# Where the projection units land in PSUM, when the block inverse starts, and how the score products are formed, in a one-core RWKV-7 and MoBA layer

## The chip, the cores and the metric

The kernel runs on one core of one Trainium2 chip. The metric is the device time of one execution in microseconds (us). In the profile PE is TensorE's matrix multiply, PEld its weight load, DVE VectorE, ACT ScalarE, POOL GpSimd and SP SyncE, whose queue issues nearly all DMAs.

## The reference

One layer on x of 512 tokens by 1024, everything in float32. Cut to what matters here:

```python
h = rms_norm(x, norm_mix_g)
proj = h @ w_in
shift_part, q_b, k_b, v_b, gate_a, gate_b = _split(proj, ...)
shift_part = token_shift_mix(shift_part, mu_shift)   # p + mu * (prev - p)
y_a = rwkv7_time_mix(...) @ w_up_a                   # 8 heads of 64
y_b = moba_attention(q_b, k_b, v_b) @ w_up_b         # 8 heads of 64, causal, ALiBi
mixed = sigmoid(gate_a) * y_a + sigmoid(gate_b) * y_b
x = x + mixed @ w_o
x = x + (silu(g_ff) * u_ff) @ w_ffn_out              # SwiGLU of rms_norm(x)
return rms_norm(x, norm_final_g)
```

`rwkv7_time_mix` is a recurrence over the tokens with a delta-rule state per head. The kernel computes it in 4 chunks of 128 tokens, which needs the inverse of a unit triangular 128 by 128 matrix for each head and chunk. `moba_attention` comes, for 512 tokens and blocks of 256, to full causal attention over 512 keys.

## The kernel before

**Products.** Big products are made from split operands. A float32 operand is held as a high part (float32r) and a low part (the rest), and `three` (L1853 to L1857) issues hi*hi, hi*lo and lo*hi into one bank of PSUM. The weights of `w_in` come in units of 128 by 1024: SP loads a unit into `wraw` (2 slots), ACT copies out the high part (`split_hi`, L860), DVE subtracts for the low part (`split_lo`, L1320), PE takes it (`take`). ACT and DVE work LEAD = 3 units ahead of PE. SP may start a load only when DVE has split the unit two before it, and ACT waits for PE to have used the unit four before.

**Stage one: 15 shift units** (u = 0 to 14: lora, k, r, v columns). For each, PE runs 24 products of 512 columns (`project`) into one bank. ACT then writes the scaled bank to SBUF (`keep_part`, L910) and DVE adds the shifted part (`shift`, L1377, it increments `mixed_ready`). Before, the units alternate between the banks 4 and 5, so unit u waits for the `shift` of unit u - 2. Between the units stand small products: `lora` (after u = 3, 4), `key_norm` (after u = 4 to 7, banks 0 and 1), `key_products` (after u = 9 and 11, banks 2, 3, 6, 7: p even and odd; L1928). ACT and DVE copy these products to `Mfull` (`m_even` L967, `m_odd` L1409).

**Block inverse.** SP stores the 32 by 32 diagonal blocks of `Mfull` to DRAM (L559) and loads them back as `Mb` (L563). DVE eliminates them in 31 steps of two TENSOR_TENSOR each (`eliminate`, L1416 and L1418), and SP takes the result `Tb` through DRAM again (L571, L575) to `Tc`. `transposed` (L1426) follows, and from `Tc` and its transpose the 128 by 128 inverses are joined per chunk. DVE's order is written out by hand. Before, the elimination comes after all 15 shifts, with one `split_lo` ahead of each of the steps 0, 9, 17 and 24.

**Stage two: v_b** (units 15 to 18, `U_VB`), 4 banks at once, one per token tile (`VB_BANK` 7, 0, 5, 6), with `gate_rows` (L2152) after the first unit and `bonus_rows` (L2159) after the third. ACT copies the four banks to `V_b` (L1068) when the last unit is done.

**Stage three: 4 chunks**, each with the masked score products of the recurrence, the joining of the inverse, the state and the outputs, filled in with the units 19 to 26 (`U_QK`, q and k of the attention) by `fill`. The unit's bank is copied to `stage` (L1075) and stored to `qk_scratch`. In chunk 0 the first things ACT does are `split_hi` of unit 22, the `stage` copy, and V_tok, B_tok and K_tok (L977). PE's `fill(c, 1, 0, 2)` waits for B_tok.

**Stage four: 16 attention steps** (4 pairs of heads p, 4 query tiles t, m = 4p + t). In each step PE runs one gate unit (5.5 us of products), `attn_scores(m + 1)` (L2221), the transposes of the weights (L2232) and the values (L2244). Before, `attn_scores` is one float32 product per head, with K = 64 (the two heads on the partitions 0 to 63 and 64 to 127) and 128 * (t + 1) columns. The profile counts two instructions for each such float32 product. q and k of a pair are loaded from DRAM to `qkT`.

After that come the up projections, `w_o`, the SwiGLU (seven-product scheme on 128 by 256 products) and the last norm, which the change does not touch.

## Time and profile before

| | |
|---|---|
| median of 3 runs | 831.39 us (830.79 to 831.90) |
| the profiled execution | 832.74 us |
| its span, first to last instruction | 831.0 us |
| granted TensorE clock | 0.998 of 2.4 GHz |
| PE busy | 811.0 us (98%) |
| DVE, ACT, POOL busy | 501.1, 339.1, 143.5 us |
| DMA | 80.08 MB, mean 96 GB/s |

The span leaves out 1.7 us of the profiled execution's time that lie before its first and after its last instruction. Busy of PE counts each product until its modelled end; successive products overlap, so the start-to-start distance of two products is shorter than the duration of one.

### The profile page before, as it was taken

To read this page: it belongs to the slowest core of one execution; us is meant where nothing else is said; L and a number is where in the kernel's file an instruction comes from. 1 tells how busy PE (TensorE), PEld (TensorE's weight loads), DVE (VectorE), ACT (ScalarE), POOL (GpSimd) and SP (SyncE) were. 2 spreads that over 40 slices of the span, in tenths; PEclk is the share of its full clock that TensorE was granted. 3 is DMA by queue.
4 is the path that set the end of the run, shared out by engine and by line. 5 is a ranking of instruction groups with operands and counts; after the bars stand their busy time and mean duration, and the time that the engine had idled before them with its cause. 6 is when DMAs were issued, how large, how long until landed. Compare 5 with 4: busy or idle time off the path is not lost.

```text
span 831.0 us, 14188 instructions
## 1 busy us (share of the span) xinstructions
PE 811.0 (98%) x5417; PEld 668.2 (80%) x5417; DVE 501.1 (60%) x772; ACT 339.1 (41%) x554; POOL 143.5 (17%) x132
## 2 busy tenths in 40 slices
PE   5999999999999999999999999999999999999997
PEld 4677777687777777777888898999999998888885
DVE  5479859553454554454762767977877876433334
ACT  6578432333325424426432443443443444333332
POOL 3063880222242101101320074000000000000000
PEclk9999999999999999999999999999999999999999
DMA  5531340511143221223254153333333313322222
GB/s 159 165 92 51 77 152 26 140 42 51 40 146 97 77 77 52 76 77 102 76 193 135 40 150 115 108 97 101 111 91 101 114 37 101 119 86 99 102 76 102
DMA packets 122578, 80.08 MB, mean 96 GB/s; under 512 B 15057, under 2 KB 110338, under 8 KB 122530
## 3 DMA queue, kind: packets, MB, share of 16 engines
q1 hardware_dynamic: 122194, 79.13, 32.1%
q8 instruction: 34, 0.56, 0.3%
q10 hardware_dynamic: 144, 0.26, 0.1%
q14 instruction: 14, 0.11, 0.0%
q0 software_dynamic: 192, 0.02, 0.0%
HBM read 74.15 MB, written 5.24 MB: 96 GB/s over the span
## 4 chain that ended last, share of the span: by engine, by line
PE 91%; DVE 4%; ACT 3%; DMA 1%; issue 1%; POOL 0%; SPq 0%; ACTq 0%; POOLq 0%; DVEq 0%
PE PS L1855 26%; PE PS L1857 25%; PE PS L1856 25%; PE PS L1955 2%; PE PS L2221 1%; PE PS L2232 1%; PE PS L2244 1%; PE PS L2054 1%; DVE sq L1394 1%; DMA xt<-in_x_dram 1%; PE PS L2152 1%; PE PS L2055 1%; DVE w_lo L1320 1%; PE PS L1874 1%; PE PS L1998 1%
## 5 line engine op out<-in xcount | busy, mean ns | idle before, releaser
L1855 PE MATMUL PS<-hT_hi,w_hi 128*128 128x512 f32 (+2 forms) x640 | 236.9, 370 | 2.8 <-DVE rkvT L1377 2.0
L1857 PE MATMUL PS<-hT_hi,w_lo 128*128 128x512 f32 (+2 forms) x640 | 229.2, 358 | 0.0
L1856 PE MATMUL PS<-hT_lo,w_hi 128*128 128x512 f32 (+2 forms) x640 | 229.2, 358 | 0.0
L1320 DVE TENSOR_TENSOR w_lo<-wraw,w_hi 128x1024 fp32r<-128x1024 f32 (+1 forms) x89 | 121.7, 1368 | 62.7 <-ACT w_hi L860 60.2
L1855 PEld LDWEIGHTS PS<-hT_hi,w_hi 128*128 128x128 f32 (+1 forms) x640 | 120.2, 188 | 28.9 <-issue 10.9
L1857 PEld LDWEIGHTS PS<-hT_hi,w_lo 128*128 128x128 f32 (+1 forms) x640 | 120.3, 188 | 19.0
L1856 PEld LDWEIGHTS PS<-hT_lo,w_hi 128*128 128x128 f32 (+1 forms) x640 | 120.4, 188 | 17.3 <-issue 1.0
L860 ACT ACTIVATE w_hi<-wraw 128x1024 fp32r<-128x1024 f32 (+1 forms) x89 | 93.1, 1047 | 64.9 <-PE PS L1857 33.4
L1855 PE MATMUL PS<-w_hi,hid_hi 128*128 128x512 f32 x176 | 68.5, 389 | 0.0
L1856 PE MATMUL PS<-w_lo,hid_hi 128*128 128x512 f32 x176 | 68.5, 389 | 0.0
L1857 PE MATMUL PS<-w_hi,hid_lo 128*128 128x512 f32 x176 | 68.5, 389 | 0.0
L1855 PE MATMUL PS<-hS,w_hi 128*128 128x256 f32 x192 | 54.3, 283 | 0.0
L1856 PE MATMUL PS<-hS,w_hi 128*128 128x256 f32 x192 | 54.3, 283 | 0.0
L1857 PE MATMUL PS<-hS,w_lo 128*128 128x256 f32 x192 | 54.3, 283 | 0.0
L1732 DVE TENSOR_TENSOR hid_lo<-hid,hid_hi 128x512 fp32r<-128x512 f32 x22 | 15.2, 691 | 58.6 <-ACT hid_hi L1220 58.6
L1220 ACT ACTIVATE hid_hi<-hid 128x512 fp32r (+1 forms) x22 | 13.9, 630 | 70.9 <-PE PS L1857 70.9
L1116 ACT ACTIVATE PT<-PS 128x128 f32<-128x128 f32 (+3 forms) x32 | 12.3, 435 | 69.1 <-PE PS L2244 67.8
L1855 PEld LDWEIGHTS PS<-w_hi,hid_hi 128*128 128x128 f32 x176 | 33.0, 188 | 6.9
L1856 PEld LDWEIGHTS PS<-w_lo,hid_hi 128*128 128x128 f32 x176 | 33.0, 188 | 6.9
L1857 PEld LDWEIGHTS PS<-w_hi,hid_lo 128*128 128x128 f32 x176 | 33.0, 188 | 6.7
L1855 PEld LDWEIGHTS PS<-hS,w_hi 128*128 128x128 f32 x192 | 36.9, 192 | 0.0
L1856 PEld LDWEIGHTS PS<-hS,w_hi 128*128 128x128 f32 x192 | 36.9, 192 | 0.0
(296 smaller groups left out, 1406.4 us busy)
## 6 DMA issues: line engine op xcount, KB each, us to landing
wraw<-in_w_in_dram SPq DMA_DIRECT2D x82, 256.0 KB, 3.1
wraw<-in_w_ffn_out_dram SPq DMA_DIRECT2D x44, 256.0 KB, 2.8
wraw<-in_w_ffn_in_dram SPq DMA_DIRECT2D x40, 256.0 KB, 3.1
pair_a<-in_w_ffn_in_dram SPq DMA_DIRECT2D x24, 256.0 KB, 3.7
pair_b<-in_w_ffn_in_dram SPq DMA_DIRECT2D x24, 256.0 KB, 3.7
wraw<-in_w_o_dram SPq DMA_DIRECT2D x16, 256.0 KB, 2.9
xt<-in_x_dram SPq DMA_DIRECT2D x4, 512.0 KB, 5.5
qk_scratch<-stage SPq DMA_DIRECT2D x8, 256.0 KB, 3.1
```

The source lines that it names most:

```text
L860: act.activation(w_hi[:, fourth % NSPL, 0:n], wraw[:, s, 0:n], ACT.Copy).then_inc(w_hi_ready, 1)
L1116: act.activation(PT[:, e].rearrange("p a b -> p (a b)")[:, 0:n], PS[:, 6 + e, 0:n], ACT.Copy)\
L1220: act.activation(hid_hi[:, r:r + 1, :], hid[:, bass.ds(k, 1), :], ACT.Copy).then_inc(acthi_ready, 1)
L1320: dve.tensor_tensor(w_lo[:, q, 0:n], wraw[:, s, 0:n], w_hi[:, q, 0:n].bitcast(F32), ALU.subtract)\
L1394: dve.reciprocal(sq[:, p, :], sq[:, p, :]).then_inc(rinv_ready, 1)
L1732: dve.tensor_tensor(hid_lo[:, r:r + 1, :], hid[:, bass.ds(k, 1), :], hid_hi[:, r:r + 1, :].bitcast(F32), ALU.subtract).then_inc(actlo_read ...
L1855: pe.matmul(out_, a_hi, b_hi, start=start, stop=False)
L1856: pe.matmul(out_, a_hi, b_lo, start=False, stop=False)
L1857: return pe.matmul(out_, a_lo, b_hi, start=False, stop=stop)
L1874: return pe.transpose(PS[:, k, t * P:(t + 1) * P], xn[:, t, k * P:(k + 1) * P], ident[:])
L1955: ins = pe.matmul(PS[:, (q + odd) % 4, i * 2 * P:(i + 1) * 2 * P], (Bt if q < 4 else Kt)[r, p, cs], kkE_R[r, p, c, :, :].rearrange("p a b ...
L1998: ins = pe.matmul(PS[HD:P, 4 + half, i * HD:i * HD + HD], MT_rb[0:HD, h, 0, HD:P], Tm[0:HD, h, :], start=True, stop=True)
```

## The change

It has four parts.

- **Banks.** The shift units go to the banks of `SHIFT_BANK` (0, 5, 4, 5, 4, 5, 6, 7, 4, 5, 0, 1, 4, 5, 4). A unit waits for the `shift` of the last unit in the same bank. Units 6 and 7 wait for the sigmoids that read the lora banks, units 10 and 11 for the `key_norm` copies of the banks 0 and 1. In the first v_b unit each of the four banks has a wait of its own, in the order of tiles 0, 1, 3, 2; in the last one the four tiles are finished one after the other, and ACT copies each as it is finished (`vb_mm`).
- **Inverse.** `m_odd` of pairs 2 and 3 goes ahead of the `split_lo` of that turn, ACT does both `m_even` before both `a_mix`. DVE leaves its shift loop after u = 12, does the shift of unit 13 and begins the elimination. The low parts of the units 16 to 20 stand ahead of the steps 3, 5, 8, 13 and 21, the shift of unit 14 ahead of step 6, the low part of unit 21 after `bonus`.
- **Score products.** q and k of a pair are loaded as `qk_raw`, split by ACT (`pair_hi`) and DVE (`pair_lo`, in place), and `attn_scores` issues hi*hi, hi*lo and lo*hi for each head, the two heads in turn, over max(128 * (t + 1), 256) columns.
- **Order of loads.** SP loads pairs 0 and 1 ahead of the store of q/k column unit 6, and pairs 2 and 3 after eight more gate loads (2 units each of k = 2 and 3, two DMAs a unit), when the last RWKV output has been split.

The diff, without context that says nothing, the new semaphores, and the renaming of `shift_bank(u)` to `SHIFT_BANK[u]`:

```diff
@@ -87,6 +87,7 @@
 VB_BANK = [7, 0, 5, 6]
+SHIFT_BANK = [0, 5, 4, 5, 4, 5, 6, 7, 4, 5, 0, 1, 4, 5, 4]
@@ -261,7 +262,11 @@
         assert at[0] == Bt_at
-        qkT = sb("qkT", [P, 2 * NP_, T])
+        qk_at = at[0]
+        qk_raw01 = sb("qk_raw01", [P, 2, 2, T])
+        qk_hi01 = sb("qk_hi01", [P, 2, 2, T], F32R)
+        at[0] = qk_at
+        qk_lo01 = sb("qk_lo01", [P, 2, 2, T], F32R)
@@ -306,6 +311,14 @@
         assert at[0] <= top
+        qk_at = at[0]
+        qk_raw23 = sb("qk_raw23", [P, 2, 2, T])
+        qk_hi23 = sb("qk_hi23", [P, 2, 2, T], F32R)
+        assert at[0] <= top
+        at[0] = qk_at
+        qk_lo23 = sb("qk_lo23", [P, 2, 2, T], F32R)
+        qk_raw, qk_hi, qk_lo = [[t[:, p] for t in two for p in range(2)]
+                                for two in ((qk_raw01, qk_raw23), (qk_hi01, qk_hi23), (qk_lo01, qk_lo23))]
...
@@ -585,8 +597,7 @@
                     sp.wait_ge(qk_stored[i], 16 * (p + 1))
-                at_ = 2 * ((p + 1) % NP_)
-                sp.dma_start(qkT[:, at_:at_ + 2, :], qk_dram[2 * p:2 * p + 2].rearrange("n p t -> p n t"))\
+                sp.dma_start(qk_raw[p], qk_dram[2 * p:2 * p + 2].rearrange("n p t -> p n t"))\
@@ -594,15 +605,19 @@
                     load_cols(U_GATE + 1, U_GATE + 1, w_in, C_GB)
+                    sp.wait_ge(score_mm, 8 * TT)
+                    for p in range(NP_ // 2):
+                        load_pair(p)
                 store_qk(n)
-            sp.wait_ge(score_mm, 8 * TT)
-            for p in range(NP_ - 1):
-                load_pair(p)
             store_qk(2 * NP_ - 1)
-            load_pair(NP_ - 1)
             load_cols(U_GATE + 3, U_GATE + 3, w_in, C_GB + P)
-            with sp.Fori(1, KD // 2) as i:
+            for m in range(2):
+                load_gates(2 + m, U_GATE + 2 * m)
+            sp.wait_ge(yalo_ready, TT)
+            for p in range(NP_ // 2, NP_):
+                load_pair(p)
+            with sp.Fori(2, KD // 2) as i:
...
@@ -1029,6 +1044,8 @@
             for u in range(N_SHIFT):
+                if u == N_SHIFT - 2:
+                    keep_part(u)
@@ -1048,11 +1065,13 @@
                         m_even(p)
+                    for p in range(u - 10, u - 8):
                         a_mix(p)
+                if u != N_SHIFT - 2:
+                    keep_part(u)
                         row_scale(p)
-                keep_part(u)
@@ -1062,9 +1081,12 @@
                         gate_out(p)
-            act.wait_ge(w_used, U_VB + 4)
             for t in range(TT):
+                if t < TT - 1:
+                    act.wait_ge(vb_mm, t + 1)
+                else:
+                    act.wait_ge(w_used, U_VB + 4)
@@ -1074,6 +1096,10 @@
                                scale=1.0 if n % 2 else -HD ** -0.5).then_inc(fill_ready, 1)
+            def pair_hi(p):
+                act.wait_ge(qk_loaded[p], 16)
+                act.activation(qk_hi[p], qk_raw[p], ACT.Copy).then_inc(qkhi_ready, 1)
@@ -1090,6 +1116,8 @@
                     split_hi(U_QK + 2 * c + 1 + LEAD, U_QK + 2 * c + 1 + LEAD)
+                else:
+                    pair_hi(0)
@@ -1133,6 +1161,8 @@
                     ya_hi(TT - 1)
+                if n in (1, 5, 6):
+                    pair_hi((1, 5, 6).index(n) + 1)
...
@@ -1502,7 +1532,14 @@
-            for u in range(N_SHIFT):
+            def pair_lo(p):
+                dve.wait_ge(qkhi_ready, p + 1)
+                dve.tensor_tensor(qk_lo[p], qk_raw[p], qk_hi[p].bitcast(F32), ALU.subtract).then_inc(qklo_ready, 1)
+            for u in range(N_SHIFT - 2):
+                if u == 12:
+                    m_odd(2)
+                    m_odd(3)
@@ -1524,20 +1561,23 @@
                     key_rows(3)
-                if u in (10, 12):
-                    m_odd(u - 10)
-                    m_odd(u - 9)
+                    m_odd(0)
+                    m_odd(1)
+            shift(N_SHIFT - 2)
             for j in range(QB - 1):
-                if j in (0, 9, 17, 24):
-                    late = (0, 9, 17, 24).index(j)
-                    split_lo(U_VB + late + LEAD, U_VB + late + LEAD)
+                if j in (3, 5, 8, 13, 21):
+                    u = U_VB + 1 + (3, 5, 8, 13, 21).index(j)
+                    split_lo(u, u)
+                if j == 6:
+                    shift(N_SHIFT - 1)
                 bonus(p)
+            split_lo(U_QK + 2, U_QK + 2)
@@ -1555,6 +1595,7 @@
                 else:
+                    pair_lo(0)
@@ -1611,6 +1652,8 @@
                     ya_lo(TT - 1)
+                if n in (1, 5, 6):
+                    pair_lo((1, 5, 6).index(n) + 1)
@@ -1919,6 +1962,8 @@
                     pe.wait_ge(m_odd_ready, p - 1)
+                elif p:
+                    pe.wait_ge(mixed_ready, 8)
@@ -2129,9 +2174,15 @@
                 take(u)
-                if u >= 3:
-                    pe.wait_ge(mixed_ready, u - 1)
-                project(u, u, shift_bank(u), GH if u in (U_LORA + 1, U_LORA + 2) else P, fresh=0 if u == 0 else None)\
+                if u in (6, 7):
+                    pe.wait_ge(sg_ready, NP_)
+                    pe.wait_ge(a_ready, NP_)
+                elif u in (10, 11):
+                    pe.wait_ge(nrm2_ready, u - 7)
+                elif u >= 3:
+                    before = max(v for v in range(u) if SHIFT_BANK[v] == SHIFT_BANK[u])
+                    pe.wait_ge(mixed_ready, before + 1)
+                project(u, u, SHIFT_BANK[u], GH if u in (U_LORA + 1, U_LORA + 2) else P, fresh=0 if u == 0 else None)\
@@ -2162,18 +2213,19 @@
                 take(u)
-                if j == 0:
-                    pe.wait_ge(nrm2_ready, NP_)
-                    pe.wait_ge(mixed_ready, N_SHIFT - 1)
-                    pe.wait_ge(m_even_ready, NP_)
-                    pe.wait_ge(m_odd_ready, NP_)
-                for kk_ in range(2):
+                steps = [(kk_, t) for kk_ in range(2) for t in ((0, 1, 3, 2) if j == 0 else range(TT))]
+                if j == 3:
+                    steps = [(kk_, t) for t in range(TT) for kk_ in range(2)]
+                for kk_, t in steps:
+                    if j == 0 and kk_ == 0:
+                        pe.wait_ge(*((m_odd_ready, NP_), (mixed_ready, 11), (mixed_ready, 14), (m_even_ready, NP_))[t])
                     w = slice(512 * kk_, 512 * kk_ + 512)
-                    for t in range(TT):
-                        ts = slice(t * P, (t + 1) * P)
-                        ins = three(PS[:, VB_BANK[t], :], hT_hi[:, k, ts], hT_lo[:, k, ts], w_hi[:, q, w], w_lo[:, q, w],
-                                    k == 0, k == KD - 1)
+                    ts = slice(t * P, (t + 1) * P)
+                    ins = three(PS[:, VB_BANK[t], :], hT_hi[:, k, ts], hT_lo[:, k, ts], w_hi[:, q, w], w_lo[:, q, w],
+                                k == 0, k == KD - 1)
+                    if j == 3 and kk_ and t < TT - 1:
+                        ins.then_inc(vb_mm, 1)
@@ -2205,9 +2257,8 @@
                 p, t = m // TT, m % TT
-                a = 2 * ((p + 1) % NP_)
                 if t == 0:
-                    pe.wait_ge(qk_loaded[p], 16)
+                    pe.wait_ge(qklo_ready, p + 1)
@@ -2216,10 +2267,15 @@
                     pe.wait_ge(G_ready, 2 * TT)
-                for e in range(2):
-                    r = slice(HD * e, HD * e + HD)
-                    pe.matmul(PS[:, 2 + 2 * (m % 2) + e, 0:P * (t + 1)], qkT[r, a, t * P:(t + 1) * P],
-                              qkT[r, a + 1, 0:P * (t + 1)], start=True, stop=True).then_inc(s_done, 1)
+                w = max(P * (t + 1), TH)
+                parts = ((qk_hi, qk_hi), (qk_hi, qk_lo), (qk_lo, qk_hi))
+                for n, (q_part, k_part) in enumerate(parts):
+                    for e in range(2):
+                        r = slice(HD * e, HD * e + HD)
+                        ins = pe.matmul(PS[:, 2 + 2 * (m % 2) + e, 0:w], q_part[p][r, 0, t * P:(t + 1) * P],
+                                        k_part[p][r, 1, 0:w], start=n == 0, stop=n == 2)
+                        if n == 2:
+                            ins.then_inc(s_done, 1)
```

## Rows read from the trace of the kernel before

**Rows 1.** The page: busy time of the engines (part 1) and two groups (part 5).

```profile
PE 811.0 (98%) x5417; PEld 668.2 (80%) x5417; DVE 501.1 (60%) x772; ACT 339.1 (41%) x554; POOL 143.5 (17%) x132
...
L1320 DVE TENSOR_TENSOR w_lo<-wraw,w_hi 128x1024 fp32r<-128x1024 f32 (+1 forms) x89 | 121.7, 1368 | 62.7 <-ACT w_hi L860 60.2
...
L860 ACT ACTIVATE w_hi<-wraw 128x1024 fp32r<-128x1024 f32 (+1 forms) x89 | 93.1, 1047 | 64.9 <-PE PS L1857 33.4
```

**Rows 2.** Timeline of PE around its waits: start us, us, instruction [idle before <-releaser].

```profile
73.59 0.39 PE L1857 MATMUL PS<-hT_hi,w_lo 128*128 128x512 f32 x1
75.35 0.47 PE L1855 MATMUL PS<-hT_hi,w_hi 128*128 128x512 f32 x1 [1.36 <-DVE rkvT L1377]
...
89.35 0.47 PE L1855 MATMUL PS<-hT_hi,w_hi 128*128 128x512 f32 x1 [0.66 <-DVE rkvT L1377]
...
113.87 0.47 PE L1855 MATMUL PS<-w_hi,hT_hi 128*128 128x512 f32 x1 [0.28 <-issue]
...
145.90 0.39 PE L1857 MATMUL PS<-w_hi,hT_lo 128*128 128x512 f32 x1
147.07 0.47 PE L1855 MATMUL PS<-hT_hi,w_hi 128*128 128x512 f32 x1 [0.78 <-ACT V_b L1068]
```

**Rows 3.** Timeline of PE: a score step of 512 columns; split products of 256.

```profile
276.88 0.39 PE L1856 MATMUL PS<-hT_lo,w_hi 128*128 128x512 f32 x1
277.10 0.39 PE L1857 MATMUL PS<-hT_hi,w_lo 128*128 128x512 f32 x1
277.42 1.13 PE L2221 MATMUL PS<-qkT 64*128 64x512 f32 x4
278.48 0.77 PE L2232 MATMUL PS<-ident,Pr 128*128 128x128 f32 x5
...
560.11 0.28 PE L1857 MATMUL PS<-hT_hi,w_lo 128*128 128x256 f32 x1
560.23 0.28 PE L1855 MATMUL PS<-hT_hi,w_hi 128*128 128x256 f32 x1
```

**Rows 4.** Timeline of DVE: key copies, shift 13, first elimination step.

```profile
93.20 1.27 DVE L1409 COPY Mfull<-PS 128x512 f32<-128x512 f32 x2
...
112.91 0.75 DVE L1377 SCALAR_TENSOR_TENSOR rkvT<-PS,par,rkvT 128x511 f32<-128x511 f32 x1 [0.52 <-ACT rkvT L910]
...
118.05 1.28 DVE L1416 TENSOR_TENSOR outer<-Mb,Tb 128x31 f32<-128x31 f32 x1
119.37 0.21 DVE L1418 TENSOR_TENSOR Tb<-Tb,outer 128x31 f32<-128x31 f32 x1
```

**Rows 5.** Timeline of PE: the second group of key products.

```profile
94.99 2.06 PE L1928 MATMUL PS<-Bt,kkE_R 64*128 64x128 f32 x32
```

**Rows 6.** Busy time by stretch: us, PE, PEld, DVE, ACT, POOL, clock, DMA.

```profile
75.40:99.00 23.60, 22.94 (x145) 18.61 (x146) 23.43 (x20) 13.57 (x19) 13.57 (x9) 1.00 0.24 68
```

**Rows 7.** Timeline of POOL: its last work before chunk 0.

```profile
111.83 7.45 POOL L744 TENSOR_TENSOR rk<-rk,rkvT 128x512 f32<-128x512 f32 x4 [0.52 <-ACT rkvT L962]
```

**Rows 8.** Timeline of SP's queue: the inverse's way back, the next weights.

```profile
145.90 0.34 SPq L571 DMA_DIRECT2D t_scratch<-Tb  x1
...
150.87 10.47 SPq L511 DMA_DIRECT2D wraw<-in_w_in_dram  x6
```

**Rows 9.** Timelines of ACT and PE in chunk 0.

```profile
155.37 1.06 ACT L860 ACTIVATE w_hi<-wraw 128x1024 fp32r<-128x1024 f32 x1 [6.98 <-DMA wraw<-in_w_in_dram]
...
158.13 0.60 ACT L977 ACTIVATE B_tok<-PS 128x512 f32<-128x512 f32 x1
...
159.26 0.50 PE L1855 MATMUL PS<-hT_hi,w_hi 128*128 128x512 f32 x1
```

**Rows 10.** Busy time by stretch: stage four, columns as in Rows 6.

```profile
257.00:382.00 125.00, 124.80 (x684) 92.08 (x682) 62.82 (x154) 51.49 (x124) 13.54 (x10) 1.00 0.28 76
```

**Rows 11.** Timelines of ACT and PE at the end of chunk 3.

```profile
252.10 0.85 ACT L1000 ACTIVATE U_sb<-PS 128x256 f32<-128x256 f32 x2 [2.33 <-PE PS L2055]
...
256.69 0.49 PE L2221 MATMUL PS<-qkT 64*128 64x128 f32 x4
```

More of the change, by code:

```diff
@@ L415, in build @@
         yalo_ready = sem("yalo_ready")
+        vb_mm = sem("vb_mm")
         vb_ready = sem("vb_ready")
@@ L419, in build @@
         qk_loaded = [sem(f"qk_loaded{i}") for i in range(NP_)]
+        qkhi_ready = sem("qkhi_ready")
+        qklo_ready = sem("qklo_ready")
         alibi_ready = sem("alibi_ready")
@@ L474, in unit_width @@
             return KD * GH if isinstance(u, int) and u in (U_LORA + 1, U_LORA + 2) else 1024
-        def shift_bank(u):
-            return 4 + u % 2 if u else 0
         def cols(bank, shape, **k):
@@ L909, in keep_part @@
                     dst, i = rkvT[:, RKV_TILE[u - U_RKV], :], RKV_TILE[u - U_RKV]
-                act.activation(dst, PS[0:np_, shift_bank(u), :], ACT.Copy, scale=omu[0:np_, i:i + 1])\
+                act.activation(dst, PS[0:np_, SHIFT_BANK[u], :], ACT.Copy, scale=omu[0:np_, i:i + 1])\
                    .then_inc(tm_ready, 1)
@@ L1376, in shift @@
                 dve.wait_ge(tm_ready, u + 1)
-                dve.scalar_tensor_tensor(out=dst[:, 1:T], in0=PS[0:np_, shift_bank(u), 0:T - 1], scalar=mu,
+                dve.scalar_tensor_tensor(out=dst[:, 1:T], in0=PS[0:np_, SHIFT_BANK[u], 0:T - 1], scalar=mu,
                                          in1=dst[:, 1:T], op0=ALU.mult, op1=ALU.add).then_inc(mixed_ready, 1)
```

## The prediction

> **What bounds the kernel now.** I read the page's busy times first: PE is busy for 98% of the span, no other engine for more than 60% [rows 1]. So a microsecond is gained only where PE stands still or where its own work shrinks, and the next view is the list of PE's waits. Behind the first loads it stands still at four places that the change touches, and the timeline of PE gives each its price [rows 2]. The bracket is measured from the modelled end of the product before. Start to start is the better ruler: two split products of 512 columns follow each other at 0.23 us (276.88 to 277.10 [rows 3]), and from 73.59 to 75.35 it is 1.76, so 1.53 us are lost where the bracket says 1.36. The bracket is short by 0.17 each time. The four places:
>
> - 75.35, for the shift of unit 7: 1.53
> - 89.35, for the shift of unit 9: 0.66 + 0.17 = 0.83
> - 113.87, start of v_b, for the shift of unit 13, which ended at 113.66 [rows 4]: 0.28 + 0.17 = 0.45
> - 147.07, first fill of chunk 0, for the first copy of V_b: 1.17 - 0.23 = 0.94
>
> Together 3.75 us. Nearly everything else that PE does is its own work.
>
> **Banks.** Unit 9 now waits for the shift of unit 5, units 10 and 11 for copies that DVE made earlier, and both first stalls go: PE would be 1.53 + 0.83 = 2.36 us ahead at the second key products, which start at 94.99 [rows 5], so at 92.63. But they write banks that DVE's first `m_odd` must have read, and that copy starts at 93.20 and ends after half of 1.27, at 93.84 [rows 4]. Can it come earlier? Between 75.4 and 99.0 DVE is busy 23.43 of 23.60 us [rows 6]; the change reorders nothing there ahead of that copy, so no. PE starts at about 93.9, and of 2.36 us 1.09 are kept. That is what stands behind the stall: DVE is the bound of this stretch, and PE waits at the next place where they meet. Units 12 to 14 then follow without a wait, as before.
>
> **v_b.** The wait at 113.87 goes, since shift 13 is now done early (below): 0.45. In the last v_b unit the first token tile is finished after a quarter of 24 * 0.227 = 5.4 us, so ACT has copied it long before PE's first fill: 0.94. PE reaches chunk 0 1.09 + 0.45 + 0.94 = 2.48 us earlier.
>
> **The inverse.** When does it begin? PE's unit 13 ends at 113.87 - 0.45 - 5.44 - 1.09 = 106.9; latency 0.3, ACT's copy 0.67, the shift 0.75: 108.6, against 118.05 [rows 4], 9.4 us earlier. But POOL still has six TENSOR_TENSOR there: two of its last key rows and the four that take 7.45 us from 111.83 [rows 7]. The first elimination instruction took 1.28 us where its equal took 0.21, and ended at 119.33, 0.05 after POOL's last (111.83 + 7.45 = 119.28) [rows 4, 7]. A DVE instruction of this kind waits for the running POOL instruction. So until POOL is done, at about 117.5, DVE gets one short instruction for each of POOL's: 3 steps in 9 us instead of 1.3, 7.6 us lost. The Trainium skill (SBUF — State Buffer, Who interferes with whom) says the same and more sharply: a VectorE instruction with two SBUF inputs and a GpSimd one that reads SBUF exclude each other for the whole instruction, and the first to issue wins. The trace agrees (1.28 against 0.21), and by that rule too the head start is nearly spent.
>
> The end of the inverse, before at 145.90 [rows 8]: -9.4, +7.6, -1.07 for the block that is no longer at step 0, +2 * 1.37 for the low parts that come in (16, 17, 18, less 21; [rows 1]), +0.75 for shift 14: 146.5. I take 146, unchanged; without the blocking it would be 139. PE does not wait for it directly, but SP does: the weights of unit 22 are loaded only behind the inverse's DMAs, at 150.87, and their high part starts at 155.37 as the first thing of ACT in chunk 0 [rows 8, 9]. Behind it stand the stage copy, V_tok and B_tok: 155.37 + 1.06 + two starts of 0.5 + 0.6, so 157.9 at the earliest, and PE's fill that waits for B_tok wants to start at 159.26 - 2.48 = 156.8. A new stall, 1.1 us at most and nothing if the inverse ends over 1.1 us earlier. I take 0.8. Stages one to three give 2.48 - 0.8 = 1.7 us.
>
> **Low parts and loads moved.** Units 16 and 17 now get their low parts at about 118 and 121, and PE takes 16 after the gate rows, at about 124.5: covered by 5 us. Shift 14 at about 122.5 is what the last gate row needs at 123: covered by 0.5 us only. The bonus products on DVE end where they did, within 0.3 us of PE's need. SP's two early loads have no wait that is not over by then, and pairs 2 and 3 have several steps.
>
> **Score products.** A step of 512 columns takes PE 278.48 - 277.10 - 0.23 = 1.15 us [rows 3]. Split products of 256 columns follow at 0.12, of 512 at 0.227 [rows 3]: 0.107 per 256 columns and 0.013 fixed. The 16 float32 products of 128 columns at 94.99 take 2.06 [rows 5], 0.26 for the two heads of a pair: four passes of 0.053 and 0.04, so the two heads run side by side, or it would be over 0.43. For 512 columns four passes are 0.853, and 0.30 is fixed. By width that is 0.51, 0.73, 0.94 and 1.15, 3.33 a pair. Now there are three passes at 256, 256, 384 and 512 columns: 0.30 + 3 * (0.12, 0.12, 0.173, 0.227) = 0.66, 0.66, 0.82, 0.98, 3.12. Four pairs: 0.85 us gained. No row has a float32r product with K = 64. Bounds: heads one after the other add 4 * 3 * 0.64 = 7.7 us, so +6.8 in all; a fixed part of 0.2 instead of 0.3 in 16 steps gives 1.6 more. I take side by side, as the float32 rows show it.
>
> The splits cost ACT 1.05 and DVE 1.37 a pair [rows 1], hidden: in the attention DVE is busy 62.8 and ACT 51.5 of 125 us [rows 10]. Uncovered they would cost 2.4 us a pair. The tightest is pair 0: `U_sb` is done at 252.95, high part 254.0, low part 255.4, needed at 256.69 [rows 11]: 1.3 us to spare.
>
> **Sum.** 831.0 - 1.7 - 0.85 = 828.45 for the span, 830.2 with the 1.7 us around it. The profiled execution is 1.35 us above the median, so the median goes from 831.39 to 828.8.
>
> **Rivals.**
>
> *The head start of PE is lost at the inverse.* POOL holds DVE longer, shift 14 is late for the gate rows (0.5 us to spare) or the inverse ends 1 to 2 us later. Each late microsecond costs PE one, and beyond 1.4 us nothing of stages one to three is left: 831.39 - 0.85 = 830.5. For it: margins of 0.3 to 0.5 us. Against it: POOL has only six instructions left. Chance 0.17.
>
> *Heads one after the other.* If float32r products of two row groups do not overlap: 831.39 - 1.7 + 6.8 = 836.5, slower. It decides once the second head adds over 0.05 us to a slot (48 slots). Against it: the same placement overlaps in float32. Chance 0.08.
>
> *Weight loads bound the short slots.* Each slot needs two weight loads. If one takes the 0.12 us of the 256-column rows and they queue, a slot is 0.24, a step 1.02, a pair 4.08 against 3.33: +3.0, 832.7. Against it: at 94.99 there are 32 products with a load each in 2.06 us, 0.064 each [rows 5]. Chance 0.05. The Trainium skill (TensorE: Matmul & The Clock Gate, LDWEIGHTS) puts a load at its columns divided by 1.2, 107 ns for 128, an estimate by which this case would be 831.6; the trace's 64 ns speaks against it.
>
> **Chances.** The forecast has 0.70. The measurement can tell 0.2%, 1.7 us. Faster by more is below 829.7: 0.70. Within: 0.20 (the lost head start and the loads case). Slower: 0.10 (the serial heads, and a piece of the others). The range takes the forecast's own bounds (all 2.48 kept and the fixed part smaller: 827.2) and the lost head start (up to 831.3).
>
> **What would show it.** Right: no wait at units 9 and 11; the second key products at 93.9 behind the Mfull copy; the first elimination instructions over 1 us each from 108.6 on, and the inverse's end within 2 us of 145.9; a wait of PE for B_tok in chunk 0; score steps of 0.66 to 0.98 us. Wrong, if PE waits between 94 and 147 elsewhere, if the short eliminations run freely, or if a score step of 512 columns takes over 1.2 us.

## The result, and the profile after

The changed kernel takes 828.07 us (median of 6 runs, 826.93 to 828.95). The kernel before, run beside it, takes 832.1 (6 runs, 830.79 to 833.31). The ratio is 0.9949, 95% interval 0.9939 to 0.996. The forecast was 828.8, range 827.2 to 831.3, from a kernel before at 831.39.

The busy times of the changed kernel, from part 1 of its page, beside [rows 1]:

```profile
PE 807.7 (98%) x5449; PEld 669.6 (81%) x5449; DVE 509.7 (62%) x776; ACT 343.5 (42%) x558; POOL 141.2 (17%) x132
```

PE is busy 3.3 us less. ACT is busy 4.4 us more, the four high parts of q and k (4 * 1.05). DVE is busy 8.6 us more, and only 5.5 of them are the four low parts (4 * 1.37). The table of PE's waits comes next (line waited for: us in total, times, longest).

```profile
PE PS L1917 <- DVE xn L1368: 8.5, 2, 8.3
PE PS L1973 <- DVE Mfull L1439: 1.5, 1, 1.5
PE PS L2374 <- DVE xn L1695: 0.4, 1, 0.4
PE PS L2288 <- DVE Pr L1626: 0.2, 1, 0.2
PE PS L1898 <- ACT B_tok L992: 0.2, 1, 0.2
```

No line waits for `rkvT` or `V_b` any more: all four stalls of [rows 2] are gone. Two waits stand where the prediction put them, at the second key products (1.5) and for `B_tok` (0.2). Neither has quite the forecast size: the prediction's numbers leave 1.3 (2.36 - 1.09) for the first and 0.8 for the second.

**A ruler.** The two traces can't be subtracted as they stand. The first product of unit 0 starts at 16.71 us before and at 14.58 after:

```profile
16.71 0.49 PE L1855 MATMUL PS<-hT_hi,w_hi 128*128 128x512 f32 x1
```

```profile
14.58 0.47 PE L1898 MATMUL PS<-hT_hi,w_hi 128*128 128x512 f32 x1
```

Those 2.13 us lie in the loading and transposing of x, which the change doesn't touch: the last 16 transposes began 1.45 us earlier (12.54 against 13.99), and the product followed their start 0.7 us sooner. In the twelve kernels below, all with the same start, that product comes anywhere from 15.46 to 18.44. So places are counted from it from here on. Four lines of PE's timeline in the changed kernel answer to [rows 5], to [rows 2] and to [rows 11]:

```profile
91.89 2.06 PE L1973 MATMUL PS<-Bt,kkE_R 64*128 64x128 f32 x32 [1.53 <-DVE Mfull L1439]
...
142.49 0.39 PE L1898 MATMUL PS<-hT_hi,w_hi 128*128 128x512 f32 x1
...
154.82 0.47 PE L1898 MATMUL PS<-hT_hi,w_hi 128*128 128x512 f32 x1 [0.19 <-ACT B_tok L992]
...
252.01 0.39 PE L2275 MATMUL PS<-qk_hi 64*128 64x256 f32 x2
```

| from the first product of unit 0, us | before | after | gain so far |
|---|---|---|---|
| second key products | 94.99 - 16.71 = 78.28 | 91.89 - 14.58 = 77.31 | 0.97 |
| first fill of chunk 0 | 147.07 - 16.71 = 130.36 | 142.49 - 14.58 = 127.91 | 2.45 |
| first score product | 256.69 - 16.71 = 239.98 | 252.01 - 14.58 = 237.43 | 2.55 |
| end of the span | 831.0 - 16.71 = 814.29 | 825.2 - 14.58 = 810.62 | 3.67 |

The change is worth 3.67 us: 2.45 before chunk 0, 0.10 in the chunks, 1.12 from the attention on. The median fell by 4.0; the 0.4 between them is small beside the spread of the start.

The inverse, on DVE, POOL and SP's queue of the changed kernel:

```profile
106.50 1.32 DVE L1446 TENSOR_TENSOR outer<-Mb,Tb 128x31 f32<-128x31 f32 x1
107.86 0.22 DVE L1448 TENSOR_TENSOR Tb<-Tb,outer 128x31 f32<-128x31 f32 x1
108.11 1.18 DVE L1446 TENSOR_TENSOR outer<-Mb,Tb 128x60 f32<-128x60 f32 x1
109.32 1.34 DVE L1448 TENSOR_TENSOR Tb<-Tb,outer 128x60 f32<-128x60 f32 x1
110.70 1.25 DVE L1446 TENSOR_TENSOR outer<-Mb,Tb 128x87 f32<-128x87 f32 x1
111.98 1.34 DVE L1448 TENSOR_TENSOR Tb<-Tb,outer 128x87 f32<-128x87 f32 x1
113.35 2.19 DVE L1350 TENSOR_TENSOR w_lo<-wraw,w_hi 128x1024 fp32r<-128x1024 f32 x1
115.47 0.26 DVE L1446 TENSOR_TENSOR outer<-Mb,Tb 128x112 f32<-128x112 f32 x1
```

```profile
109.29 5.18 POOL L759 TENSOR_TENSOR rk<-rk,rkvT 128x512 f32<-128x512 f32 x4
```

```profile
142.48 0.34 SPq L583 DMA_DIRECT2D t_scratch<-Tb  x1
```

The first step begins at 91.92 instead of 101.34 on the ruler, 9.4 us earlier. Until POOL's multiplications end (109.29 + 5.18 = 114.47) five of the six short instructions take 1.18 to 1.34 us. The low part of 2.19 us spans that end, and behind it the next short instruction takes 0.26. The inverse is stored at 127.90 instead of 129.19, so 1.3 us are left of the 9.4.

### The profile page after: what moved, and what is told of

Read it like the earlier page. It is cut to its first block, busy times and chain, and to the rows that moved or that the text cites. A ratio compares the mean times of both kernels' runs of the same rounds, so it can differ in the third digit from the quotient of the medians.

```text
span 825.2 us, 14239 instructions
## 1 busy us (share of the span) xinstructions
PE 807.7 (98%) x5449; PEld 669.6 (81%) x5449; DVE 509.7 (62%) x776; ACT 343.5 (42%) x558; POOL 141.2 (17%) x132
## 4 chain that ended last, share of the span: by engine, by line
PE 90%; DVE 5%; ACT 2%; DMA 1%; issue 1%; POOL 0%; SPq 0%; ACTq 0%; POOLq 0%; DVEq 0%
PE PS L1898 26%; PE PS L1899 25%; PE PS L1900 25%; PE PS L2000 2%; PE PS L2288 1%; PE PS L2300 1%; PE PS L2275 1%; PE PS L2099 1%; DVE sq L1424 1%; DVE w_lo L1350 1%; PE PS L2203 1%; DMA xt<-in_x_dram 1%; PE PS L2100 1%; PE PS L2043 1%; PE PS L2073 1%
```

## Experiments

All twelve derive from the changed kernel. The ratio is to the kernel before, run beside each (its medians are 831.82 to 832.45 us). Places are from the first product of unit 0, as above, and each is the start of its row less that of the first product, in one trace of each kernel. "Key products" are the two groups of small products behind the units 9 and 11, "inverse stored" is the start of SP's store of `Tb`.

| kernel | median us | ratio to before (95%) | first product | first key products | second key | first fill | inverse stored | first score | end |
|---|---|---|---|---|---|---|---|---|---|
| before | 832.1 | 1 | 16.71 | 64.26 | 78.28 | 130.36 | 129.19 | 239.98 | 814.29 |
| after | 828.07 | 0.9949 (0.9939 to 0.996) | 14.58 | 62.61 | 77.31 | 127.91 | 127.90 | 237.43 | 810.62 |
| float32 scores | 830.08 | 0.997 (0.9958 to 0.9982) | 16.04 | 62.59 | 77.32 | 127.90 | 127.86 | 237.37 | 811.66 |
| head by head | 828.75 | 0.9958 (0.9943 to 0.9973) | 16.08 | 62.61 | 77.31 | 127.91 | 127.88 | 237.46 | 810.72 |
| exact width | 828.15 | 0.9946 (0.9932 to 0.9959) | 16.81 | 62.73 | 77.44 | 128.02 | 127.98 | 237.80 | 810.79 |
| two banks | 829.21 | 0.9968 (0.9956 to 0.998) | 15.69 | 64.22 | 78.25 | 128.83 | 127.91 | 238.33 | 811.51 |
| late inverse | 830.28 | 0.9974 (0.9963 to 0.9985) | 18.44 | 62.84 | 77.53 | 128.13 | 129.44 | 238.67 | 811.86 |
| quiet POOL | 828.8, one run | | 16.44 | 62.64 | 77.34 | 127.92 | 123.72 | 237.43 | 810.66 |
| copy first | 828.22 | 0.9956 (0.9942 to 0.9969) | 16.36 | 63.03 | 76.62 | 127.20 | 128.45 | 238.27 | 811.44 |
| copy first, early load | 827.29 | 0.9938 (0.9925 to 0.9952) | 16.47 | 62.64 | 76.24 | 126.81 | 127.82 | 236.29 | 809.43 |
| early load | 828.71 | 0.9958 (0.9944 to 0.9971) | 15.46 | 62.59 | 77.29 | 127.91 | 127.91 | 237.44 | 810.64 |
| all three | 826.66 | 0.9937 (0.9924 to 0.9951) | 15.63 | 62.63 | 76.20 | 126.78 | 127.85 | 236.25 | 809.27 |
| old last unit | 830.24 | 0.9969 (0.9956 to 0.9982) | 17.05 | 62.86 | 77.59 | 129.17 | 128.21 | 238.72 | 811.95 |
| late inverse, early load | 829.03 | 0.9957 (0.9942 to 0.9973) | 16.41 | 62.60 | 77.31 | 127.88 | 129.19 | 237.59 | 810.79 |

The column of the first key products is a second landmark. Up to there all but before and "two banks" run the same work, yet "late inverse", "old last unit" and "copy first" carry 0.23 to 0.42 us from unit 0, whose first one or two products take longer in these three traces. It is taken off where their later places are read. An interval is 0.9 to 1.3 us to each side, so the medians alone could not tell most of these kernels apart. The places agree within 0.1 us where nothing differs, but for such starts (0.12 in "exact width" too) and for the wait for `B_tok`, which varies by up to 0.4 us. The expected times below were reckoned from 828.07; most medians came 0.1 to 1.4 us above them, about as much as the intervals are wide, so the expectations are held against the places.

### Float32 score products

```diff
-                w = max(P * (t + 1), TH)
-                parts = ((qk_hi, qk_hi), (qk_hi, qk_lo), (qk_lo, qk_hi))
-                for n, (q_part, k_part) in enumerate(parts):
-                    for e in range(2):
-                        ...
+                w = P * (t + 1)
+                for e in range(2):
+                    r = slice(HD * e, HD * e + HD)
+                    pe.matmul(PS[:, 2 + 2 * (m % 2) + e, 0:w], qk_raw[p][r, 0, t * P:(t + 1) * P],
+                              qk_raw[p][r, 1, 0:w], start=True, stop=True).then_inc(s_done, 1)
```

> The changed kernel with each head's score product as one float32 product again, of the exact width, and without the high and low parts of q and k (loads, banks and order as changed). My theory: the attention gives back what three passes for four had saved: a step of 512 columns goes from 0.98 to 1.15 us, one of 128 from 0.66 to 0.51, and the stretch from the first score step to the last is 0.85 to 1.1 us longer; the time is 828.9 to 829.2 us. Rival: the gain of the attention comes from other moves (loads and gate copies in another order), then the stretch stays as in the changed kernel within 0.2 us.

From the first score product to the end it takes 811.66 - 237.37 = 574.29 us, the kernel before 574.31, the changed kernel 573.19. So this stretch is 1.10 us longer than in the changed kernel, as expected (0.85 to 1.1), and the end is 1.04 later on the ruler; the median is higher than expected, 830.08. The edit takes out the splits with the products, so the 1.1 us are the products less whatever the splits cost, and the other moves of loads and copies give nothing. The steps of PE alone give 1.04 (below), so the splits cost nothing that shows.

### Head by head

```diff
-                for n, (q_part, k_part) in enumerate(parts):
-                    for e in range(2):
+                for e in range(2):
+                    for n, (q_part, k_part) in enumerate(parts):
```

> The same six products of a score step, but the three of head 0 first and then the three of head 1, so that neighbours use the same 64 rows. My theory: two products lie side by side only where neighbours use different halves of the rows; a slot of two heads then costs twice its pass, a step of 512 columns 3 * 0.227 = 0.68 us more, of 384 0.52, of 256 0.36; a pair 1.9 us, four pairs 7.7 us, the time about 835.8 us. Rival: the order within a step makes no difference (the overlap is not one of neighbours), the time stays at 828.1.

My expectation fell. The end stands at 810.72, 0.1 from the changed kernel and far from the 7.7 us. Here are a step of 512 columns on PE and its weight loads. The program's order is three products of head 0 and then three of head 1:

```profile
273.79 0.39 PE L1900 MATMUL PS<-hT_hi,w_lo 128*128 128x512 f32 x1
274.11 0.50 PE L2275 MATMUL PS<-qk_hi 64*128 64x512 f32 x2
274.44 0.40 PE L2275 MATMUL PS<-qk_lo,qk_hi 64*128 64x512 f32 x2
274.68 0.40 PE L2275 MATMUL PS<-qk_hi,qk_lo 64*128 64x512 f32 x2
275.01 0.87 PE L2288 MATMUL PS<-ident,Pr 128*128 128x128 f32 x6
```

```profile
274.11 0.19 PEld L2275 LDWEIGHTS PS<-qk_hi 64*128 64x128 f32 x2 [0.35 <-issue]
274.22 0.20 PEld L2275 LDWEIGHTS PS<-qk_lo,qk_hi 64*128 64x128 f32 x2
274.45 0.19 PEld L2275 LDWEIGHTS PS<-qk_hi,qk_lo 64*128 64x128 f32 x2
```

Each row holds two instructions, one of each head: both heads load and multiply the same part together, although two other products stand between them in the program. The first product of head 1 starts 0.010 us behind the first of head 0 (0.003 where they are neighbours) and over 0.2 us before the second of head 0. The step takes 275.01 - 273.79 = 1.22 us, as with the heads interleaved (1.21). Each half of the rows runs its own sequence, and the order across halves didn't matter here. The Trainium skill (TensorEngine Tiling (Array Packing), Key Properties) says that different tiles can load weights and multiply in parallel, and the trace agrees: two heads, one slot of 0.24 us. The rival of serial heads, which I gave 0.08, doesn't come about in either order.

### Exact width of the first score product

```diff
-                w = max(P * (t + 1), TH)
+                w = P * (t + 1)
```

> The score products of the first tile of each pair take 128 columns instead of being widened to 256. By columns (0.107 us for 256 and 0.013 fixed) a pass falls from 0.12 to 0.067 us, 0.16 a pair and 0.65 us in all: 827.4 us. Rival: a float32r product of 128 columns is slower by column than one of 256; were it as slow as float32 (four passes of 0.053), a slot would take 0.22, 0.3 us more a pair and 1.3 us more in all: 829.4 us.

From the first score product to the end it takes 572.99 us against 573.19: 0.2 gained, not 0.65 and not a loss. The end itself stands no earlier (810.79), because the first score product came 0.37 us later in this trace, behind a slower start (0.12) and a wait of 0.6 for `B_tok`; the median is 828.15, not 827.4. Here are the step of 128 columns on PE and its loads:

```profile
282.82 0.39 PE L1900 MATMUL PS<-hT_hi,w_lo 128*128 128x512 f32 x1
283.14 0.33 PE L2275 MATMUL PS<-qk_hi 64*128 64x128 f32 x2
283.30 0.28 PE L2275 MATMUL PS<-qk_lo,qk_hi 64*128 64x128 f32 x2
283.41 0.28 PE L2275 MATMUL PS<-qk_hi,qk_lo 64*128 64x128 f32 x2
283.62 1.09 PE L2288 MATMUL PS<-ident,Pr 128*128 128x128 f32 x8
```

```profile
283.13 0.19 PEld L2275 LDWEIGHTS PS<-qk_hi 64*128 64x128 f32 x2 [0.35 <-issue]
283.24 0.19 PEld L2275 LDWEIGHTS PS<-qk_lo,qk_hi 64*128 64x128 f32 x2
283.35 0.19 PEld L2275 LDWEIGHTS PS<-qk_hi,qk_lo 64*128 64x128 f32 x2
```

The products follow at 0.16 and 0.11, where 256 columns gave 0.22 and 0.12. The loads follow at 0.11 and 0.11 here; at 256 columns the third came 0.12 behind the second, at the pace of the products. I read from this that at 128 columns the load sets the slot. Only the first product gains by the smaller width: a step takes 0.80 us instead of 0.87.

This corrects a step of the prediction. I had divided the 2.06 us of [rows 5] by 32 loads, read 0.064 us for one and held it against the figure of the Trainium skill (TensorE: Matmul & The Clock Gate, LDWEIGHTS: columns divided by 1.2, 107 ns for 128). But those 32 loads ran in the two halves of the rows side by side. Here one load takes 0.11, and the trace agrees with that figure. The rival failed for another reason: a slot's two loads don't queue, and 0.11 lies just under the 0.12 of 256 columns. The prediction's 831.6 let the two loads of a slot queue: that premise failed, not the figure.

### Two banks

```diff
-SHIFT_BANK = [0, 5, 4, 5, 4, 5, 6, 7, 4, 5, 0, 1, 4, 5, 4]
+SHIFT_BANK = [0, 5, 4, 5, 4, 5, 4, 5, 4, 5, 4, 5, 4, 5, 4]
...
-                if u in (6, 7):
-                    ...
-                elif u >= 3:
+                if u >= 3:
```

> The changed kernel with the projection units alternating between two PSUM banks again, each waiting for the shift before the last (unit 0 in bank 0). My theory: both stalls return (1.5 at unit 7, 0.8 at unit 9), but the 1.5 us that PE waits at the second key products for the copy of Mfull goes, so PE loses only 0.9 to 1.1 us by there and the same at the end: 829.1 us. Rival: the copy moves with the banks as well and all 2.36 us are lost: 830.4.

The two stalls are back (2.0 us in the table of waits) and the wait at the second key products is gone:

```profile
PE PS L1898 <- DVE rkvT L1407: 2.0, 2, 1.4
```

The second key products come at 78.25, 0.94 later than in the changed kernel, and the end 0.89 later. Of 2.36 us of stall, the further banks return 0.9. The copy of `Mfull` sits at 76.45 with two banks and at 76.48 with the six of `SHIFT_BANK`: DVE bounds this stretch.

### Late inverse

```diff
-            for u in range(N_SHIFT - 2):
+            for u in range(N_SHIFT):
...
-                if j in (3, 5, 8, 13, 21):
-                    u = U_VB + 1 + (3, 5, 8, 13, 21).index(j)
-                    split_lo(u, u)
-                if j == 6:
-                    shift(N_SHIFT - 1)
+                if j in (0, 9, 17, 24):
+                    late = (0, 9, 17, 24).index(j)
+                    split_lo(U_VB + late + LEAD, U_VB + late + LEAD)
```

(The shift of unit 13 and the low part of `U_QK + 2` behind the bonus fall away as well.)

> The changed kernel with the inverse begun behind the last shift again and with the low parts of units 16 to 21 where they were before the change (banks, split of the last v_b unit and score products as changed). My theory: POOL's multiplications had taken most of the head start, so without it the inverse ends only about 1.3 us later, counted from the first product of unit 0 (129.2 instead of 127.9 us), and PE loses 0.45 at the start of v_b for shift 13 and waits up to 1 us more for B_tok: 0.5 to 1.3 us in all, 828.6 to 829.4. Rival: the head start of some 10 us is real, the inverse ends 7 us or more later and PE loses 5 us or more.

With the 0.23 us of the start taken off, the inverse is stored 1.3 us later and the first score product comes 1.0 later; PE waits 1.2 us for `B_tok` instead of 0.2. The 0.45 us at the start of v_b didn't return, although shift 13 is late again. Shift 13 on DVE and the first product of v_b on PE:

```profile
114.24 0.73 DVE L1407 SCALAR_TENSOR_TENSOR rkvT<-PS,par,rkvT 128x511 f32<-128x511 f32 x1
```

```profile
114.43 0.39 PE L1894 MATMUL PS<-w_hi,hT_hi 128*128 128x512 f32 x1
```

The product starts 0.5 us before the shift ends, and without a wait: each token tile there now waits for its own bank, and the tile in the bank of unit 13 is taken last. The head start of 9.5 us (first step at 101.4 instead of 91.9, with the 0.23 off) is worth 1.3 on DVE and 1.0 on PE.

### Quiet POOL

```diff
-                pool.tensor_tensor(rk[:, p, :], rk[:, p, :], rkvT[:, p, :], ALU.mult).then_inc(rk_ready, 1)
+                pool.memset(rk[:, p, :], 0.0).then_inc(rk_ready, 1)
```

> POOL's four multiplications of rk by r for the bonus are replaced by memsets of the same tiles; this leaves the bonus term out of the result. My theory: they exclude DVE, so the elimination's short instructions that took 1.2 to 1.3 us beside them take 0.2 to 0.3, the low part beside them 1.4 instead of 2.2, and the inverse ends about 4 us earlier (counted from the first product of unit 0: 124 instead of 127.9); PE gains at most the 0.19 us that it waits for B_tok. Rival: the first steps are long for a reason of their own (first use of the tiles, chained waits), and stay over 1 us.

This kernel leaves the bonus term out of the result, and there is one time and one trace of it. DVE and POOL:

```profile
108.61 1.18 DVE L1448 TENSOR_TENSOR Tb<-Tb,outer 128x31 f32<-128x31 f32 x1
109.82 1.33 DVE L1446 TENSOR_TENSOR outer<-Mb,Tb 128x60 f32<-128x60 f32 x1
111.19 0.22 DVE L1448 TENSOR_TENSOR Tb<-Tb,outer 128x60 f32<-128x60 f32 x1
111.44 0.25 DVE L1446 TENSOR_TENSOR outer<-Mb,Tb 128x87 f32<-128x87 f32 x1
```

```profile
108.38 1.32 POOL L746 TENSOR_TENSOR rk<-aT,rkvT 128x512 f32<-128x512 f32 x1
109.78 1.29 POOL L748 TENSOR_TENSOR Kt<-rk,Kt 128x512 f32<-128x512 f32 x1
111.13 0.99 POOL L759 MEMSET rk<- 128x512 f32 x2
```

Beside POOL's last two TENSOR_TENSOR the short instructions take 1.18 and 1.33 and end 0.08 to 0.09 us behind them; beside the memsets they take 0.22 and 0.25. The inverse is stored 4.2 us earlier (4 expected), and PE gains nothing: 810.66. Its 0.19 us for `B_tok` is gone, but it waits 0.3 for `TmT`, a tile of the joining of the inverse in chunk 0, a little further on. That wait has the same 0.3 whether the inverse is stored at 123.72 (here) or at 129.19 ("late inverse, early load"), so it isn't a wait for the end of the elimination. The exclusion is shown, and also that in this range nothing of PE behind `B_tok` hangs on when the inverse is stored. The Trainium skill (SBUF — State Buffer, Who interferes with whom) says that a VectorE instruction with two SBUF inputs contends with a GpSimd one that reads SBUF and not with one that only writes it; the trace agrees on both halves.

### Copy first, with and without the early load, and the early load alone

On DVE the low part of unit 13 goes behind the copies. On SP unit 22's weights go ahead of the inverse's transfers:

```diff
-                split_lo(u + LEAD, u + LEAD)
+                if u != 10:
+                    split_lo(u + LEAD, u + LEAD)
...
                     m_odd(0)
                     m_odd(1)
+                    split_lo(u + LEAD, u + LEAD)
```

```diff
-            for n in range(3):
+            for n in range(4):
                 load_qk(n)
...
             for n in range(3, 2 * NP_):
-                load_qk(n)
+                if n > 3:
+                    load_qk(n)
```

> The changed kernel with DVE's low part of unit 13 behind the key rows 2 and 3 and the first two copies of Mfull instead of ahead of them. The wait of 1.5 us at the second key products goes, since the copy comes 1.9 us earlier. My theory: the gain doesn't last, since the weights of unit 22 come no earlier: the wait for B_tok in chunk 0 grows from 0.2 to 1.2 to 1.7 us, and the time is 827.6 to 828.1. Rival: the inverse and with it the load move up as far as PE does, the gain of 1.5 us stays: 826.6.

> As the run with the copy first, and SP issues the weights of unit 22 ahead of the transfers of the inverse instead of behind them. My theory: no wait for B_tok is left in chunk 0, so the 1.5 us of the second key products stay, and the 0.2 for B_tok comes on top: 826.4 us. Rival: the copies of B_tok wait for something other than the high part of unit 22 (the inverse itself, or PE's transposes), then the time is that of the run without the early load.

> The changed kernel with the weights of unit 22 loaded ahead of the inverse's transfers, and nothing else. My theory: only the wait of 0.19 us for B_tok is there to be gained, the first score step comes 0.1 to 0.2 us earlier counted from the first product of unit 0 (237.3), and the time is 827.9 us: the load helps only a PE that is ahead. Rival: the early load is worth the 1.7 us by which the run with the copy first and the early load came ahead of the one with the copy first alone; then 826.6.

*Copy first.* PE's wait at the second key products falls to 0.4. The copy came 1.1 us earlier, not 1.9: without the low part ahead of them, the two key rows on DVE ran beside POOL and took 3.0 us instead of 2.4:

```profile
89.19 3.04 DVE L1433 TENSOR_TENSOR kkE_R<-kk,kkE_R 128x512 f32<-128x512 f32 x2
92.16 1.27 DVE L1439 COPY Mfull<-PS 128x512 f32<-128x512 f32 x2
```

PE's waits of this kernel:

```profile
PE PS L1900 <- ACT B_tok L992: 1.8, 1, 1.8
...
PE PS L1975 <- DVE Mfull L1439: 0.4, 1, 0.4
```

The gain is not only lost, as I expected, but overpaid: with the 0.42 of the start off, the first fill comes 1.1 us earlier and the first score product 0.4 us later than in the changed kernel. The inverse is stored where it was (128.0), since POOL's multiplications end later too, and ACT's high part of unit 22 starts 0.6 us later.

*With the early load* the wait for `B_tok` is gone and the 1.1 us stay: first score product 1.14 earlier, end 1.19 earlier. I had expected 1.7, from a copy 1.9 earlier. *The early load alone* gains nothing (810.64 against 810.62; I had expected 0.1 to 0.2). Its waits show why: the 0.2 for `B_tok` went to `TmT`, a little further on.

```profile
PE PS L1974 <- DVE Mfull L1440: 1.5, 1, 1.5
...
PE PS L2044 <- ACT TmT L1001: 0.3, 1, 0.3
```

So the same edit is worth 0 or 1.6 us: 0 where PE comes late, and 811.44 - 0.39 - 809.43 = 1.6 where PE has been made early (0.39: 63.03 - 62.64, the difference of the starts).

### All three

Copy first, early load and exact width together.

> Copy of Mfull first, early load and exact width of the first score product together. The gains of the single runs add: 1.19 us for the first two and 0.25 for the width, the span from the first product of unit 0 is 809.2 us (810.6 in the changed kernel) and the time about 827.0. Rival: the pairs' first step is not on the path any longer, or the waits move, and the time stays at 827.3 or more.

809.27 on the ruler, 1.35 less than the changed kernel (1.44 expected), median 826.66. It is the fastest kernel of the study, 5.0 us under before on the ruler. Against the changed kernel the ruler shows the gain; the intervals of the ratios (0.9924 to 0.9951 and 0.9939 to 0.996) overlap.

### Old last unit

```diff
-                if j == 3:
-                    steps = [(kk_, t) for t in range(TT) for kk_ in range(2)]
...
-                if t < TT - 1:
-                    act.wait_ge(vb_mm, t + 1)
-                else:
+                if t == 0:
                     act.wait_ge(w_used, U_VB + 4)
```

> The last v_b unit in its old order (all four token tiles finished at its end) and the copies of V_b behind its end. My theory: PE's first fill of chunk 0 waits 0.94 us for the first copy again; 0.2 of it were spent at B_tok anyway, so the first score step is 0.75 us later than in the changed kernel (238.2 from the first product) and the time is 828.8. Rival: the copies behind it delay ACT's high part of unit 22 and B_tok too, then 0.94 or more are lost.

With 0.25 of the start off, the first fill is 1.0 us later (0.94 expected), as PE waits 0.8 for `V_b` again, and the first score product is 1.0 later too, where I had expected 0.75. Nothing of it was absorbed at `B_tok`: that wait went, but the 0.3 for `TmT` came. The rival had the size (0.94 or more), but not the reason: ACT's high part of unit 22 started no later. The split of the last unit is worth its full 0.94 to 1.0 us.

### Late inverse with the early load

> The late inverse of the earlier run (begun behind the last shift, low parts in their old places) together with the early load of unit 22. My theory: the late inverse cost 1.0 us only through the load that stood behind it in SP's queue, so with the load ahead of it the time is that of the changed kernel within 0.3 us (first score step 237.4 to 237.8 from the first product; 828.1 to 828.4). Rival: PE waits for the inverse's own tiles (Tc, Tm or TmT) by then, and the 1.0 us stays: 238.4 and 829.1.

The inverse is stored at 129.19, as in the kernel before, and the first score product comes at 237.59, the end at 810.79: 0.16 and 0.17 behind the changed kernel, where the late inverse alone lost 1.0. My expectation held (237.4 to 237.8). So the path from the inverse to PE ran through SP's queue, to within 0.2 us. One load moved gives nearly all that the rearranged inverse gave.

## Why the prediction was right

The median came 0.7 us under the forecast, and every wait and step that the prediction priced stands where it said. The sizes are less exact than the median makes it look: on the ruler the gain is 3.67 us where the steps sum to 2.55. By its steps:

**Banks** (2.36 removed, 1.09 kept at the second key products). Right in mechanism, a little high in size: the second key products come at 77.31, 0.97 earlier and not 1.09, and the copy at 76.48 against 76.49 before. "Two banks" shows 0.94 for this part alone, and "copy first" that DVE's order held the rest.

**v_b** (0.45 + 0.94). PE is 2.45 us ahead at the first fill, 2.48 predicted. "Old last unit" gives the second term as 1.0. The first term came, but its reason was only half the matter: I put it down to shift 13 being done early, and "late inverse" shows that the waits by bank remove the stall even with shift 13 late.

**The inverse** (begins 9.4 us earlier, 7.6 lost to POOL, ends unchanged). The mechanism is right, shown by "quiet POOL"; the term was 1.4 us too large. The first step began at 91.92 (108.6 - 16.71 = 91.9 predicted). From there to 115.47 - 14.58 = 100.89, 9.0 us, DVE did six short instructions and a low part, free 6 * 0.23 + 1.37 = 2.75: so 6.2 lost, not 7.6. Most of that is POOL: its multiplications ended at 99.89 on the ruler, where I had put 117.5 - 16.71 = 100.8. The low part was issued before that end and done 1.1 us behind it, where I had let it take 1.37. The inverse ended 1.3 us earlier than before on the ruler; the prediction's sum (146.5) is 1.9 later than that, and the 0.5 beyond this term was not looked into.

**The wait for B_tok** (0.8 taken, 0 to 1.1 given). This is the term that was mis-sized: 0.19, because of those 1.3 us. The prediction said that nothing would be left if the inverse ended over 1.1 us earlier; a little was left, since the chain from the store to ACT's high part took 9.7 us instead of 9.5. Stages one to three gave 2.55, not 1.7. The 0.10 us gained beyond the first fill fits the 0.3 for `TmT`, a wait of the kernel before that is gone, less the 0.19. (The terms given for `B_tok` add to 158.0, not to 157.9.)

**Score products** (0.85). Measured 1.04 from the steps. A step of 512 columns takes 1.21 from the last projection product to the transposition, as predicted (0.98 + 0.23); for 256 columns 0.87 against 0.89, for 384 1.03 against 1.05. Here is one of 256:

```profile
280.25 0.39 PE L1900 MATMUL PS<-hT_hi,w_lo 128*128 128x512 f32 x1
280.57 0.38 PE L2275 MATMUL PS<-qk_hi 64*128 64x256 f32 x2
280.80 0.28 PE L2275 MATMUL PS<-qk_lo,qk_hi 64*128 64x256 f32 x2
280.91 0.28 PE L2275 MATMUL PS<-qk_hi,qk_lo 64*128 64x256 f32 x2
281.12 1.09 PE L2288 MATMUL PS<-ident,Pr 128*128 128x128 f32 x8
```

Pairs 1 to 3 take 3.98 us for their four steps, 4.24 before: 0.26 a pair, 0.21 predicted. The splits were hidden, as said: no line of PE waits for them.

**The base.** The sum started from a median of 831.39; the six runs of before beside the result gave 832.1. On the ruler the change was forecast at 1.7 + 0.85 = 2.55 and measured at 3.67: 1.1 us more, 0.85 of it from the chunks' wait and the rest from the score products. The higher base hid part of that, which is luck and not merit. The lower end of the range was not fully worked out either: both bounds named for it together give 831.39 - 2.48 - 0.85 - 1.6 = 826.5, not 827.2; of the 1.6 for a smaller fixed part the steps show 0.24 (3.98 us a pair where 3.12 + 4 * 0.23 = 4.04 was predicted).

**Rivals.** The lost head start didn't come: shift 14 and the low parts were on time. Serial heads and queued loads are excluded, both by a fact that I had half read, that the two halves of the rows run on their own.

## What to carry to other kernels

Look past a stall that is removed for the next place where the engines meet: 2.36 us of stall gave 0.9, and the engine that bounds the stretch names the next edit. An early start is worth what it moves at the end of the chain: trace the result's way to the bound engine, queue by queue. Here it led through a load that only stood behind the inverse's transfers in SP's queue, and moving that load did nearly as much as rearranging the inverse. And count from a landmark behind the noisy start: it resolved 0.1 to 0.4 us in single traces, where the medians' intervals were about 2 us wide.

## What the runs showed of the hardware

- The two halves of PE's rows proceed on their own: with three products of one half ahead of three of the other in the program, both halves ran together, at 0.24 us for two heads of 512 columns.
- A weight load of 128 columns in half the rows takes 0.11 us, and two of different halves run side by side. A split product of 128 columns in a run costs 0.11, hardly less than one of 256 (0.12).
- Beside a two-input instruction of POOL, DVE's short ones (two inputs too) took 1.2 to 1.3 us instead of 0.2 in five cases of six (changed kernel), and ended about 0.1 us behind it; a memset of POOL's held nothing up.
- From the store of the inverse to ACT's high part of unit 22 (two transfers and a load in a row) it took 9.5 us before (155.37 - 145.90), 9.7 after (152.16 - 142.48), and in the eight others without the early load from 9.2 ("old last unit", 154.42 - 145.26) to 10.15 ("copy first", 154.96 - 144.81). The wait for `B_tok` followed it where nothing else differed: 0.2 after, 0.4 in "head by head" (9.9), 0.6 in "exact width" (10.1). So a wait behind a chain of transfers has a spread of its own, and the four kernels with the early load show no wait for `B_tok` at all.
- The first product of unit 0 started between 14.58 and 18.44 us in fourteen traces of kernels with the same start.
